# The order of the twelve matmuls in a product of a hybrid HGRN2 and pooling block

## The reference

```python
h = rms_norm(z, norm_w[l])
p = (h @ w_in[l] + b_in[l]).astype(f32)          # 8 matrices of 1024 x 1024
q, fz, iv, g_hg, u, g_pool, m_hg, m_pool = jnp.split(p, split_at, axis=-1)
...                                              # gated linear recurrence on q, fz, iv -> o
y_hg = (o * jax.nn.silu(g_hg)) @ w_down_hg[l]
...                                              # causal window means of u -> pooled
y_pool = (mixed * pool_scale[l] * jax.nn.silu(g_pool)) @ w_down_pool[l]
merged = jax.nn.sigmoid(m_hg) * y_hg + jax.nn.sigmoid(m_pool) * y_pool
z = z + merged @ w_out[l]
return rms_norm(z, final_norm_w)[:, N_META:]
```

## Time and profile before

| | |
|---|---|
| median of three runs | 1060.2 us |
| the profiled execution's own time | 1060.07 us |
| its span, first to last instruction | 1058.3 us |
| TensorE (PE) busy | 1027.6 us, 97% of the span |
| VectorE (DVE) busy | 782.2 us, 74% |
| ScalarE (ACT) busy | 491.9 us, 46% |
| share of the chain of waits on PE | 82% |
| share of it on DVE | 12% |
| matmuls high x high in products (acc bank) | 1112 |
| mean granted TensorE clock | 0.998 |

### The profile page before, as it was taken

One profiled execution on the slowest core, in us unless ns is written; L12 is line 12 of the kernel. 1 busy time (PEld: TensorE's weight loads), 2 busy tenths in 40 slices (PEclk: granted clock), 3 DMA queues, 4 the chain that ended last, 5 costly groups with the idle time before them and its releaser, 6 DMA issues.

```text
span 1058.3 us, 18484 instructions
## 1 busy us (share of the span) xinstructions
PE 1027.6 (97%) x7252; PEld 837.8 (79%) x7252; DVE 782.2 (74%) x1277; ACT 491.9 (46%) x833; POOL 96.9 (9%) x164
## 2 busy tenths in 40 slices
PE   7889999999999999999999999999999999999997
PEld 6667888888888887878888887788887787787886
DVE  7888787878787878787676877864569789889234
ACT  7663545454535353544353433444457346246222
POOL 2500010101010101010101010011100110000111
PEclk9999999999999999999999999999999999999999
DMA  7022020202020202021312122228322674465233
GB/s 263 1 79 81 22 81 21 81 21 81 20 81 22 79 23 73 29 89 63 100 41 90 60 90 80 70 88 298 117 95 100 232 285 154 160 189 181 79 105 129
DMA packets 36054, 104.60 MB, mean 99 GB/s; under 512 B 4576, under 2 KB 4576, under 8 KB 35968
## 3 DMA queue, kind: packets, MB, share of 16 engines
q1 hardware_dynamic: 22064, 65.61, 19.1%
q0 software_dynamic: 8240, 26.79, 6.9%
q10 hardware_dynamic: 5664, 11.02, 2.9%
HBM read 78.23 MB, written 25.17 MB: 98 GB/s over the span
## 4 chain that ended last, share of the span: by engine, by line
PE 82%; DVE 12%; issue 3%; ACT 2%; DMA 1%; POOL 0%; DVEq 0%; ACTq 0%; POOLq 0%
PE acc L1178 68%; PE levels L1318 2%; DVE w_lo L1547 2%; PE levels L1178 1%; PE miscs L1340 1%; PE miscs L1351 1%; PE miscs L1352 1%; PE acc L1222 1%; DVE r_lo L2084 1%; DMA gate_in<-smh_spill 1%; PE miscs L1178 1%; DVE att L1703 1%; PE acc L1366 1%; PE miscs L1295 1%; PE miscs L1358 1%
## 5 line engine op out<-in xcount | busy, mean ns | idle before, releaser
L1178 PE MATMUL acc<-r_hi,w_hi 128*128 128x512 f32 x1112 | 445.6, 401 | 13.7 <-DVE w_lo L1547 5.6
L1178 PE MATMUL acc<-r_hi,w_lo 128*128 128x512 f32 x1112 | 434.1, 390 | 0.0
L1178 PE MATMUL acc<-r_lo,w_hi 128*128 128x512 f32 x1112 | 433.9, 390 | 0.0
L1178 PEld LDWEIGHTS acc<-r_hi,w_hi 128*128 128x128 f32 x1112 | 208.8, 188 | 69.4 <-issue 22.4
L1178 PEld LDWEIGHTS acc<-r_hi,w_lo 128*128 128x128 f32 x1112 | 208.7, 188 | 45.0
L1178 PEld LDWEIGHTS acc<-r_lo,w_hi 128*128 128x128 f32 x1112 | 209.1, 188 | 39.8
L696 ACT ACTIVATE w_hi<-sum 128x512 fp32r<-128x512 f32 x156 | 97.8, 628 | 163.4 <-PE acc L1178 82.5
L1547 DVE TENSOR_TENSOR w_lo<-sum,w_hi 128x512 fp32r<-128x512 f32 x156 | 106.3, 685 | 56.9 <-ACT w_hi L696 56.6
L1547 DVE TENSOR_TENSOR w_lo<-raws,w_hi 128x512 fp32r<-128x512 f32 x120 | 82.0, 686 | 62.9 <-ACT w_hi L696 62.9
L696 ACT ACTIVATE w_hi<-raws 128x512 fp32r<-128x512 f32 x120 | 74.5, 624 | 27.1 <-PE acc L1178 27.1
L1178 PE MATMUL acc<-wo_hi,m_hi 128*128 128x512 f32 x128 | 49.9, 390 | 0.6 <-DVE wo_lo L2220 0.6
(11 more groups left out here) (298 smaller groups left out, 1365.1 us busy)
## 6 DMA issues: line engine op xcount, KB each, us to landing
raws<-in_wstream SPq DMA_DIRECT2D x88, 512.0 KB, 3.6
xin<-in_x SPq DMA_DIRECT2D x8, 512.0 KB, 6.1
a_spill<-gt POOLq DMA_DIRECT2D x16, 256.0 KB, 3.5
c_spill<-pg POOLq DMA_DIRECT2D x16, 256.0 KB, 2.8
stage<-a_spill ACTq DMA_DIRECT2D x4, 1024.0 KB, 14.1
smh_spill<-zq POOLq DMA_DIRECT2D x16, 256.0 KB, 2.4
gate_in<-smh_spill SPq DMA_DIRECT2D x16, 256.0 KB, 5.6
part_spill<-zq POOLq DMA_DIRECT2D x16, 256.0 KB, 5.1
```

Source lines behind the costliest of these rows:

```text
L1178: ins = pe.matmul(out_ap, a, b, start=first and n == 0, stop=final and n == 2, skip_group_check=partial)
```

## The change: the order in a product, and its waits

A product's twelve matmuls are no longer issued step by step in threes. The four of high parts come first, n = 0 to 3. Then, in pair 0 and in pairs 32 and 36, come the four with low weights and last the four with the low operand; in all other pairs first those with the low operand and last those with low weights. Part 0 of a product is now n = 0 to 5 and part 1 is n = 6 to 11. At the start of a product TensorE waits for w_hi, and in pairs 0, 32 and 36 for the operand's high part; (0, 5) still waits for h_lo. The wait for w_lo, and that for the operand's low part, stand before the first matmul that reads it.

```diff
-            def operands_ready(p, i):
-                pe.wait_ge(S["w_lo"], POS[p, i] + 1)
-                if p == 0 and i < 2:
-                    pe.wait_ge(S["h_lo"], 4)
+            def high_parts_ready(p, i):
+                pe.wait_ge(S["w_hi"], POS[p, i] + 1)
+                if p == 0 and i == 0:
+                    pe.wait_ge(S["h_hi"], 4)
+                elif p == 0 and i == 1:
+                    pe.wait_ge(S["h_copied"], 4)
                 elif p == 0 and i == 5:
                     pe.wait_ge(S["h_lo"], CHUNKS)
                     pe.wait_ge(S["h_copied"], CHUNKS)
                 elif p == 0:
-                    sem, count = {2: ("v6_lo", 2), 3: ("v5_lo", 1), 4: ("v7_lo", 2), 6: ("v4_lo", 2)}[i]
-                    pe.wait_ge(S[sem], count)
+                    pe.wait_ge(S[{2: "v6_hi", 3: "v5_hi", 4: "v7_hi", 6: "v4_hi"}[i]], 1 if i == 3 else 2)
+                elif p in (P_DH, P_DP):
+                    pe.wait_ge(S["r_hi"], 7 * ((p - P_DH) // 4) + i + 1)
+
+            def weights_low_ready(p, i):
+                pe.wait_ge(S["w_lo"], POS[p, i] + 1)
+
+            def operand_low_ready(p, i):
+                if p == 0 and i in (0, 1):
+                    pe.wait_ge(S["h_lo"], 4)
+                elif p == 0 and i != 5:
+                    pe.wait_ge(S[{2: "v6_lo", 3: "v5_lo", 4: "v7_lo", 6: "v4_lo"}[i]], 1 if i == 3 else 2)
                 elif p in (P_DH, P_DP):
                     pe.wait_ge(S["r_lo"], 7 * ((p - P_DH) // 4) + i + 1)
...
-                    operands_ready(p, i)
+                    high_parts_ready(p, i)
...
-                for k in (2 * part, 2 * part + 1):
+                operand_last = p == 0 or p in (P_DH, P_DP)
+                for n in range(6 * part, 6 * part + 6):
+                    k = n % KH
                     w = slice(k * P, (k + 1) * P)
-                    ins = three(bank[:, :], (w_hi[slot][:, w], w_lo[slot][:, w]), (r_hi[i][:, k, :], r_lo[i][:, k, :]),
-                                i in (0, 1, 5 if p < EARLY else 3) and k == 0, k == KH - 1, True)
+                    weights, moving = w_hi[slot][:, w], r_hi[i][:, k, :]
+                    if n // KH == (1 if operand_last else 2):
+                        if k == 0:
+                            weights_low_ready(p, i)
+                        weights = w_lo[slot][:, w]
+                    elif n // KH:
+                        if k == 0:
+                            operand_low_ready(p, i)
+                        moving = r_lo[i][:, k, :]
+                    ins = pe.matmul(bank[:, :], weights, moving, start=n == 0 and i in (0, 1, 5 if p < EARLY else 3),
+                                    stop=n == 3 * KH - 1, skip_group_check=True)
                 if part == 1:
                     ins.then_inc(S["mm_done"], 1)
```

## The result

The changed kernel takes 1061.8 us (median of 13 executions, 1061.1 to 1063.7), the kernel before 1060.2 us in the same series (13 executions, 1059.2 to 1061.5). The ratio is 1.0020, 95% interval 1.0012 to 1.0027. It is slower by 1.6 us. That is inside the range on record (1056.9 to 1062.2), but the forecast was 1059.8 us, a small gain, and the change is a small loss.

The account below looks back on a forecast made before the run. TensorE was taken as the bound, busy 1027.6 of 1058.3 us. Start -0.9, down_hg +0.8 and down_pool -0.2 sum to -0.3 us from 1060.07, forecast 1059.8 us, range 1056.9 to 1062.2 (own range by the bounds 1058.7 to 1061.6).

Parts of the forecast that it names:

- The change to down_hg: Pair 32: TensorE's 1.9 us lead lost waiting at (33,6); earlier c_spill loads slow gate_in: +0.8 us, bounds 0 and 1.9.
- down_pool: Pair 36: (36,6) ends 1.8 us sooner, but (37,6) waits for VectorE's addition behind pt_in: -0.2 us, bounds 0 and 1.8.
- What bounds the kernel: Whole kernel: TensorE busy 1027.6 of 1058.3 us; 14.9 us of data waits in three places, nearly all such idle time.
- the order: Every product: still 12 matmuls and 12 weight loads of the same forms, so the new order costs 0 us.
- the waits: All 280 products: satisfied waits at the start and inside a product taken as 0 us; other bound 22 us.
- The start: Products (0,0) to (2,0): TensorE restarts 1.2 us sooner at (2,0), 0.9 us remain: -0.9 us, bounds 0.35 and 1.2.
- its cap: Scan matmuls at 86.73 us need a VectorE instruction that moves by only 0.35 us, so 0.9 of 1.2 us remain.
- the even share: Between 830 and 841 us load streams share evenly, so 1.8 us more overlap costs gate_in 0.9 us; 0.8 taken.
- rival 1: At (33,6): a 3.1 us stop brings half clock for 3.4 us, costing 1.7 us; 1061.5 us in all; chance 0.20.
- Rival 2: At (33,6) and (37,6): early gate_in or pt_in keeps 1.9 or 1.8 us; 1057.4 or 1055.5 us; chance 0.19.
- Rival 3: All 280 products: even a satisfied wait inside a product costs a 0.08 us restart; 22 us, 1082 us; chance 0.04.
- rival 4: Whole kernel: high and low parts arrive together, so the change does nothing; 1060.1 us; chance 0.07.

Follow-up runs that it names:

- order alone: New matmul order everywhere, but every product waits for high and low parts at its start, against the kernel before: 1060.7 us, ratio 1.0009.
- the start alone: New order and waits in pairs 0 to 31 only, pairs 32 to 39 old, against the kernel before: 1058.3 us, ratio 0.9984.
- the four cases above: Kernel before, changed kernel with c_spill loads held, changed kernel, kernel before with c_spill loads early: gate_in 8.36, 7.52, 10.69 and 12.92 us.
- c_spill early: Kernel before, old order, with only the first two stage<-c_spill loads one product earlier in ScalarE's list: 1066.4 us, ratio 1.0059.
- the old form in pair 32: Changed kernel, but pair 32 keeps the old order and old waits: 1057.2 us, ratio 0.9973 against the kernel before; its profiled execution took 1061.2 us.
- the 19 matmuls in place of the stop: Changed kernel with 19 unused matmuls before TensorE's wait for add_22(33): 1060.1 us, and 1059.3 us when run again.
- pair 36 alone: Kernel before with the new order and waits in pair 36 only: 1059.1 us, ratio 0.9989.
- pair 32 alone: Kernel before with the new order and waits in pair 32 only: 1064.3 us, ratio 1.0038.
- c_spill held in the changed kernel: Changed kernel where ScalarE waits for VectorE's third gate multiplication before the first two stage<-c_spill loads: 1057.5 us, ratio 0.9975 against the kernel before.

## Why the prediction was wrong

The sum had -0.3 us, the profiled executions +1.5 us. Two terms failed. The clock, which the sum had at 0, cost 1.6 us. The change to down_hg, which it had at +0.8 us, cost 2.2. Either error alone turns the small gain into a loss. Two errors went the other way: down_pool gave 0.85 us more than forecast, and 0.54 us lie ahead of every product. That the time fell inside the range is partly luck: without down_pool's error it would have been about 1062.7 us.

*What bounds the kernel, the order, the waits.* Right for the stretch where it can be read. The order is free between 85 and 840 us (order alone). Satisfied waits inside a product cost nothing that can be seen: from the scan matmuls to (31,6) the changed kernel takes 714.75 us (85.20 to 799.95), the one before 714.60 (86.73 to 801.33), with some 200 products between.

*The start, -0.9 us.* Right, with its cap: 0.84 us in the two profiled traces, 0.86 to 1.03 with the start alone. (2,0) came 1.2 us sooner against VectorE (52.48 us behind its instruction of 25.03 instead of 53.68), and the scan matmuls 1.0 us. The 1.4 us between the two traces at (31,6) hold another 0.54 us from ahead of the first product. There executions differ: kernels with the old start reached that VectorE instruction between 25.03 and 25.74 us.

*Down_hg, +0.8 us: the first step that failed, in its size.* Its mechanism was right in each link: c_spill is let go early by TensorE, gate_in takes longer, VectorE's addition stands behind it, TensorE takes all of its lead and more as a stop. It cost 2.2 us, beyond even my upper bound of 1.9 (gate_in took 2.33 us longer, less 0.15 us that other links gave back). I moved the c_spill transfer by the 1.8 us by which its issue moves against gate_in. But before, 4.5 us passed from issue to the first packet (none of q10 among the packets of 831.18 to 835.5 us), and now 2.5 us. The 16 engines were 71% busy in the 2 us ahead of the issue before, and 16% now. From 827.95 to 832.2 us:

```profile
q1 hardware_dynamic: 216, 0.41, 36.6%
q0 software_dynamic: 118, 0.42, 24.2%
q10 hardware_dynamic: 70, 0.14, 16.6%
```

The first packets came at 830.5 instead of 835.7 us: 5.2 us sooner, 3.7 of them against the load of gate_in (which itself moved by 1.5). The Trainium skill ("DMA: Bandwidth & Descriptors", section "Queues, rings and completion order") says that a DMA engine takes turns between the queues that have work, a packet at a time. By that rule what counts is when a queue begins to have packets and not when its load is issued; that q10's amount per us rises with gate_in's time in the four cases above agrees.

How much each us of earlier packets costs is not settled. Half of 3.7 us gives 1.8, not far from the 2.3 us by which gate_in took longer. But with c_spill early in the old kernel the packets came 5.4 us sooner against gate_in, half of which is 2.7, and gate_in took 4.6 us longer; and in the execution of 1061.2 us of the old form in pair 32 they came only 0.4 us sooner, and gate_in took 2.1 us longer. So the even share is my estimate, and these runs don't bear it out as a rule.

*The clock, rival 1 (0.20): the second step that failed.* It happened and cost 1.6 us (priced at 1.7), as the 19 matmuls in place of the stop show. Here the reasoning contradicted itself. The rival was said to decide from a stop between 1.8 and 2.4 us, and the forecast's own terms already made a stop of 3.1 us; the only argument against it, that TensorE is dense around it, had no row. By its own numbers it belonged in the forecast, which would then have read 1061.5 us, near the 1061.8 measured. Some of that nearness is luck, since the other errors nearly cancel.

*Down_pool, -0.2 us.* Wrong, though within its bounds: -1.05 us in these traces, -1.4 with pair 36 alone. "VectorE's work after 903 us, which has no gap" overlooked the 1.10 us at 915.89 that TensorE itself caused. The forecast's own range also left this term's bound out: with 0 and -1.8 us for down_pool its lower end is -3.0 us and not -1.4.

Rival 2 did not happen at down_hg but did at down_pool, in part. Rival 3 would have cost 22 us, and its stretch shows 0.15; rival 4 falls with the 0.84 us of the start.

## What to carry to other kernels

A wait that is shortened lets go whatever is queued behind it, on every engine: look for the large transfer whose issue hangs on the work that gets faster, and for the small one that somebody waits for beside it. Look at when packets begin to flow, not only at the time of issue; here a load issued before the engines filled also started sooner. How much the collision costs had to be measured. When a forecast's own sum holds a stop as long as one that cost the clock elsewhere in the trace, the clock belongs in the sum. A load that gates only an engine's own later work should not stand ahead of the addition for which TensorE waits.

## What the runs showed of the hardware

- The length of a stop alone does not decide whether the clock falls. At (33,6) full clock followed a stop of 1.51 us, half clock one of 2.51 us (the old form in pair 32, 0.53 over 3.4 us) and those of 4.26, 4.39 and 4.82 us. At the start a stop of 2.37 us before the product at 52 us was followed by half clock before, and the same stop, also 2.37 us, in the kernel with pair 36 alone by none:

```profile
52.32 0.47 PE L1178 MATMUL levels<-r_hi,w_hi 128*128 128x512 f32 x1 [2.37 <-DVE w_lo L1569]
```

```profile
51.00:56.00 5.00, 3.26 (x13) 2.46 (x14) 4.52 (x6) 1.49 (x3) 0.00 (x0) 1.00 0.00 0
```

- Shorter stops at the start were followed by half clock too: 1.88 us with c_spill held in the changed kernel (a half from 67.4 to 70.8 us), while the stop of 2.57 us before the product at 51.22 us in the same trace was not, and 1.90 us with the order alone. Stops of 1.85 and 1.86 us at the same product in the other new kernels were not (seven kernels). So the edge of rival 1, between 1.8 and 2.4 us, is not a bound:

```profile
66.24 1.16 PE L1290 MATMUL acc<-r_hi,w_hi 128*128 128x512 f32 x4 [1.88 <-ACT w_hi L696]
```

- Half clock lasted 3.4 us at the start of the kernel before and at both places of the changed one. It lasted 6.8 us with the stop of 4.26 us (842.1 to 848.9, pair 32 alone) and with that of 4.82 us (845.7 to 852.5, c_spill early), and there it began inside the stop. The twelve matmuls of (33,6) then took 4.96 and 5.28 us to the next product, where 2.85 us pass at full clock in the kernel before.
- The c_spill loads on ScalarE's queue took 4.1 to 4.5 us from issue to the first packet where the DMA engines had been 70 to 94% busy in the 2 us ahead of the issue (six kernels), and 1.7 to 2.7 us where they had been 1 to 27% busy (four kernels).
